# Four accumulator banks for the projection, and a new order of the last head's output projection, in a two-layer attention trunk

## The chip, the cores and the metric

The kernel runs on one core of one Trainium2 chip. The metric is the device time of one execution in microseconds (us). It was run three times before the change: 563.05, 563.07 and 563.96 us, median 563.07 us.

A core has a matrix engine (PE, which loads weights as PEld and multiplies as PE), a vector engine (DVE), an activation engine (ACT), a general engine (POOL) and a queue that starts transfers (SP). Each runs its own instruction list in order; the lists meet only at semaphores. PE writes its sums into eight banks (PSUM, 128 partitions of 512 floats each), which DVE and ACT read and write and POOL does not touch in this kernel.

## The reference, cut to what matters

```python
D_MODEL = 1024; SEQ = 512; DEPTH = 2; N_HEADS = 8; HEAD_DIM = 128
for i in range(DEPTH):                     # layer 0: MoBA with rotary; layer 1: forgetting attention
    hdn = rms_norm(x, norm_g[i])
    if i == 0:
        q, k, v, z = split(hdn @ a_w_in[0], 4)
        q = apply_rope(rms_norm(split_heads(q), a_q_norm)); k = apply_rope(rms_norm(split_heads(k), a_k_norm))
        y = moba_attention(q, k, v)        # two blocks of 256 and top-1 of the past block: plain causal attention
    else:
        q, k, v, z, f = parts of hdn @ b_w_in[0]
        log_f = log_sigmoid(f + b_f_bias); c = cumsum(log_f)
        q = rms_norm(q, b_q_norm); k = rms_norm(k, b_k_norm)
        y = softmax(causal(q @ k.T * d**-0.5 + c_q - c_k)) @ v
    x = x + (merge_heads(y) * silu(z)) @ w_out[i]
```

All products are computed in three matrix multiplications each (high part by high part, high by low, low by high), so that 32-bit inputs keep their precision.

## The kernel before, in words

The 512 tokens are four tiles of 128. A layer's input, normalised and turned, stays in `hT_hi` and `hT_lo`. The work goes head by head. For head h+1, `qkv` projects the four tiles: tile t is 24 matmuls of 384 columns (q, k and v) into one bank, and `zproj` is 24 matmuls of 512 columns for the gate z. ACT squares and sums q and k of a tile and copies v (`read_qkv`), POOL makes the reciprocal root (`rstd_qk`), and DVE applies it, with the rotation in layer 0 (`norm_qk`), and takes v's low part (`split_v`). When the four tiles are done, DVE turns q and k by 16 transposes into the two banks from QT_BANK (`turn_qk`), ACT and DVE split them into high and low parts (`split_qk`), and PE computes the scores of the head (`scores`) into banks 3, 4 and 5. DVE takes the row maxima (`maxima`), ACT the exponentials (`exps`), DVE inverts the sums (`invert_sums`), ACT scales (`normalise`), PE turns the probabilities (`turn_probs`) into banks 3, 4 and 5 again, ACT and DVE split them (`split_probs`), and PE multiplies by v (`values`, bank 3). DVE multiplies the result by the gate (`gate_y`), ACT and DVE split it (`split_y`, `low_y`).

Every engine has the same outer form (`heads_loop`): `first` for head 0's projection, one `period` written out, a loop of six more periods, and `last` for head 7. In period h PE does, in this order: the projection of head h+1's tiles 0 and 1, the scores of h, tiles 2 and 3, the turn of h's probabilities, z of h+1, the values of h. DVE's order is in `period` from line 1010, ACT's from line 723, POOL's from line 1144; they are fixed by hand and nothing overtakes.

Banks before: the projection alternates between banks 0 and 1 (head 0 of layer 0 has four), so tile t waits until `norm_qk` of tile t-2 has been through its bank. 2 is z, 3 is values and scores of tile 3, 4 and 5 the other scores, 6 and 7 the turned queries and keys. The statistics `ssq`, `rstd` have two slots. FORGET_BANK (4) is used once, at the head of layer 1.

`last` (PE line 532, DVE 1029, ACT 739) has no projection of a next head to set beside head 7's attention. In its place stand parts of the output projection: column half 0 for tiles 0, 1, 2, 3, of which the contributions of heads 0 to 6 can be summed early (a `project` for one tile and one head k is three matmuls of 512 columns), and head 7's contribution when `ylo_set` reports its low part. ACT in `last` converts weight chunks of the second half (`split_w`, four raw buffers): chunk 4 needs the buffer of chunk 0, which is loaded again when POOL has made chunk 0's low part.

Of the kernel before, what the change touches and what calls it, by code (L numbers as in the profile page):

```python
# [51 lines left out]
def build_trunk(nc, x, norm_g, w_out, a_w_in, a_q_norm, a_k_norm, b_w_in, b_f_bias, b_q_norm,  # L52
                b_k_norm, rope_cos, rope_sin, out):
    with ExitStack() as ctx:
# [42 lines left out]
        ssq = sb("ssq", [P, 2, 2])  # L97
        msq = sb("msq", [P, 2, 2])
        rstd = sb("rstd", [P, 2, 2])
# [7 lines left out]
        Z_BANK, Y_BANK, QT_BANK = 2, 3, 6  # L107
# [81 lines left out]
        def qkv_bank(layer, h, t):  # L189

            return (0, 1, 3, 4)[t] if layer == 0 and isinstance(h, int) and h == 0 else t % 2
# [7 lines left out]
        def turn_bank(layer, t):  # L199

            return 3 if layer == 0 and t == 1 else QT_BANK

        def unit_bank(c, t):

            return QT_BANK if c == 0 and t == 3 else t
# [6 lines left out]
                      (QT_BANK, t, slice(cols.start + CH // 2, cols.stop))]  # L212
# [125 lines left out]
        def _(pe):  # L338
# [51 lines left out]
            def qkv(layer, h, slot, t):  # L390

                a = TILES * (HEADS * layer + h) + t
                wait(pe, qkn_set, a - 1)
                if isinstance(a, int) and a == TILES:
                    for k in range(KC):
                        first_w(1, k)
                        qkv_part(layer, h, slot, t, (k,))
                    return
                if t == 0:
                    pe.wait_ge(wlo_set, KC * (JOBS * layer + h + 1))  # L400
                qkv_part(layer, h, slot, t, range(KC))
# [130 lines left out]
            def last(layer):  # L532
                g = HEADS * (layer + 1)
                u = TILES * OUT_CHUNKS * layer
                h = HEADS - 1

                pe.wait_ge(wlo_set, KC * (JOBS * layer + HEADS + 1))
                pe.wait_ge(ylo_set, g - 2)
                pe.wait_ge(qkn_set, TILES * g)
                project(layer, 0, 0, range(6), True, False)  # L540
                project(layer, 0, 1, range(2), True, False)
                scores(layer, h, 1)
                project(layer, 0, 1, range(2, 6), False, False)
                pe.wait_ge(ylo_set, g - 1)
                project(layer, 0, 0, [6], False, False)
                project(layer, 0, 1, [6], False, False)
                project(layer, 0, 3, range(5), True, False)
                turn_probs(layer, h)
                project(layer, 0, 3, range(5, 7), False, False)
                pe.wait_ge(gate_set, g)  # L550
                project(layer, 0, 2, range(3), True, False)
                values(layer, h, 1)
                project(layer, 0, 2, range(3, 7), False, False)
                pe.wait_ge(ylo_set, g)
                for t in range(TILES):
                    project(layer, 0, t, [h], False, True)
                pe.wait_ge(wlo_set, KC * (JOBS * layer + HEADS + 2))
                for t in range(TILES):
                    pe.wait_ge(x_added, u + 1 + t)
                    if layer + 1 == LAYERS and t == TILES - 1:  # L560
                        for part in out_parts[-2:]:
                            project_part(*part)
                    else:
                        project(layer, 1, t, range(HEADS), True, True)
                    if layer + 1 < LAYERS and t >= 1:
                        turn_hidden(layer + 1, t - 1)
# [6 lines left out]
        def _(act):  # L573
# [45 lines left out]
            def read_qkv(layer, h, s, t):  # L619
# [3 lines left out]
                wait(act, rstd_set, a - 1)  # L623
                wait(act, ssq_set, a)
                for m in range(2):
                    sq = act.activation(junk[:, m, :], banks[:, qkv_bank(layer, h, t), m * P:(m + 1) * P],  # L626
                                        ACT.Square, scale=SCALE, accum_out=ssq[:, t % 2, m:m + 1])
# [132 lines left out]
        def _(dve):  # L760
# [57 lines left out]
            def norm_qk(layer, h, t):  # L818
# [4 lines left out]
                if layer == 1:  # L823
                    for m in range(2):
                        last = dve.scalar_tensor_tensor(out=qkn[:, t, m, :], in0=banks[:, qkv_bank(layer, h, t), m * P:(m + 1) * P],
                                                        scalar=rstd[:, t % 2, m:m + 1], in1=cos_t[:, 0, m, :],
# [3 lines left out]
                for m in range(2):  # L830
                    swapped = banks[:, qkv_bank(layer, h, t), m * P:(m + 1) * P].rearrange("p (a n) -> p a n", a=2)[:, ::-1, :]
                    dve.scalar_tensor_tensor(out=rot[:, t % 2, m].rearrange("p (a n) -> p a n", a=2), in0=swapped,
                                             scalar=rstd[:, t % 2, m:m + 1],
# [3 lines left out]
                for m in range(2):  # L837
                    part = banks[:, qkv_bank(layer, h, t), m * P:(m + 1) * P]
                    dve.scalar_tensor_tensor(out=part, in0=part, scalar=rstd[:, t % 2, m:m + 1], in1=cos_t[:, t, m],
# [5 lines left out]
            def turn_qk(layer, h):  # L845

                g = HEADS * layer + h
                dve.wait_ge(qkn_set, TILES * (g + 1))
                for a in range(QUADS):
# [179 lines left out]
            def last(layer):  # L1029
                h = HEADS - 1  # L1030
                begin(layer, h)
                silu_part(layer, h, 0)
                maxima(layer, h)
                silu_part(layer, h, 1)
                invert_sums(layer, h)
                for n in range(2, 4):
                    silu_part(layer, h, n)
# [20 lines left out]
        def _(pool):  # L1058
# [17 lines left out]
            def rstd_qk(layer, h, t):  # L1076
                a = TILES * (HEADS * layer + h) + t
                pool.wait_ge(ssq_set, a + 1)
                wait(pool, qkn_set, a - 1)
                pool.tensor_tensor(msq[:, t % 2, :], ssq[:, t % 2, :], eps[:, :], ALU.add).then_inc(msq_set, 1)  # L1080
                pool.wait_ge(msq_set, a + 1)
                pool.tensor_tensor(rstd[:, t % 2, :], msq[:, t % 2, :], power[:, :], ALU.pow).then_inc(rstd_set, 1)  # L1082
# [122 lines left out]
```

## Time and profile before

| | us |
|---|---|
| median of three runs | 563.07 |
| the profiled execution, its own time | 564.51 |
| its span, first to last instruction | 562.5 |
| PE busy / PEld busy | 545.7 / 499.9 |
| DVE busy | 408.6 |
| ACT busy | 286.6 |
| POOL busy | 294.1 |

The busy time of PE is over matmuls that overlap each other, and their ends are modelled, so 97% does not mean that PE loses only 3%. A view that lists waits says for each engine which instruction waited and what released it; the view in order of time gives start, duration, engine, source line and operation, and in square brackets the idle time before it and its releaser. Most of the span is made of fourteen nearly equal periods, seven in each layer, and of two `last` sections, which begin near 236 us and 510 us.

### The profile page before, as it was taken

How to read it: one execution, taken by the hardware profiler on the slowest of the kernel's cores; microseconds unless marked ns; L12 is line 12 of the kernel's file. 1: busy time of each engine (PE TensorE's matmuls, PEld its weight loads, DVE VectorE, ACT ScalarE, POOL GpSimd, SP SyncE). 2: the span in 40 equal slices, each digit the busy share in tenths (PEclk: the TensorE clock that was granted, in tenths of full speed). 3: DMA queues.
4: the chain of work that ended last, by engine and by line, in shares of the span. 5: the costliest groups of instructions: out<-in, count | busy, mean ns of one | idle time of the engine just before them, and what ended most of it. 6: DMA issues, size and time to landing. Idle time of an engine off the chain costs nothing.

```text
span 562.5 us, 9740 instructions
## 1 busy us (share of the span) xinstructions
PE 545.7 (97%) x2958; PEld 499.9 (89%) x2958; DVE 408.6 (73%) x1039; ACT 286.6 (51%) x841; POOL 294.1 (52%) x348
## 2 busy tenths in 40 slices
PE   6998999999999999999999989999999999999998
PEld 4997999999999999878888989999999999998887
DVE  3799797979797979774363767787869595959321
ACT  5735555555454546453445463736464647373500
POOL 4854545454544444425545576657475756663700
PEclk9999999999999999999999999999999999999999
DMA  9812323131313131204442334423341535141221
GB/s 280 215 49 87 93 58 95 56 95 56 93 56 93 56 93 56 93 8 130 108 102 76 95 90 80 95 76 79 90 112 56 118 50 131 37 131 37 76 93 57
DMA packets 78237, 49.95 MB, mean 89 GB/s; under 512 B 4089, under 2 KB 71417, under 8 KB 78210
## 3 DMA queue, kind: packets, MB, share of 16 engines
q1 hardware_dynamic: 78208, 49.61, 32.6%
q8 instruction: 14, 0.23, 0.2%
q14 instruction: 13, 0.11, 0.1%
q10 hardware_dynamic: 2, 0.00, 0.0%
HBM read 47.48 MB, written 2.11 MB: 88 GB/s over the span
## 4 chain that ended last, share of the span: by engine, by line
PE 52%; DVE 17%; POOL 12%; issue 12%; ACT 3%; DMA 2%; SPq 1%; POOLq 0%; ACTq 0%; DVEq 0%
PE banks L343 14%; PE banks L345 14%; PE banks L344 14%; DVE banks L853 11%; POOL w_lo L1064 8%; PE banks L458 3%; POOL rstd L1082 3%; DVE pT_lo L894 2%; PE banks L444 2%; PE banks L375 1%; DMA w_raw<-in_b_w_in_dram 1%; POOL msq L1080 1%; DMA first_raw<-in_a_w_in_dram 1%; ACT junk L626 1%; PE banks L433 1%
## 5 line engine op out<-in xcount | busy, mean ns | idle before, releaser
L1064 POOL TENSOR_TENSOR w_lo<-w_raw,w_hi 128x512 fp32r<-128x512 f32 x147 | 188.4, 1300 | 94.8 <-ACT w_hi L590 94.8
L343 PE MATMUL banks<-w_hi,hT_hi 128*128 128x384 f32 x512 | 175.2, 342 | 8.7 <-DVE qkn L842 4.6
L345 PE MATMUL banks<-w_hi,hT_lo 128*128 128x384 f32 x512 | 172.2, 336 | 0.0
L344 PE MATMUL banks<-w_lo,hT_hi 128*128 128x384 f32 x512 | 172.2, 336 | 0.0
L853 DVE STREAM_TRANSPOSE banks<-qkn 32x256 f32<-32x256 f32 x256 | 116.6, 456 | 3.5
L343 PEld LDWEIGHTS banks<-w_hi,hT_hi 128*128 128x128 f32 x512 | 96.8, 189 | 13.1 <-DVE qkn L842 7.3
L590 ACT ACTIVATE w_hi<-w_raw 128x512 fp32r<-128x512 f32 x148 | 87.8, 643 | 21.8 <-DMA w_raw<-in_b_w_in_dram 13.9
L344 PEld LDWEIGHTS banks<-w_lo,hT_hi 128*128 128x128 f32 x512 | 97.0, 189 | 0.7
L345 PEld LDWEIGHTS banks<-w_hi,hT_lo 128*128 128x128 f32 x512 | 96.8, 189 | 0.0
L1080 POOL TENSOR_TENSOR msq<-ssq,eps 128x2 f32<-128x2 f32 x64 | 13.9, 218 | 125.0 <-ACT junk L626 125.0
L919 DVE RECIPROCAL gz<-gz 128x128 f32<-128x128 f32 x64 | 58.1, 928 | 0.0
L626 ACT ACTIVATE junk<-banks 128x128 bf16<-128x128 f32 x128 | 34.1, 276 | 41.2 <-PE banks L345 41.1
L635 ACT ACTIVATE qkT_hi<-banks 128x512 fp32r<-128x512 f32 x32 | 17.4, 596 | 72.5 <-DVE banks L853 72.5
L343 PE MATMUL banks<-w_hi,yT_hi 128*128 128x512 f32 (+1 forms) x136 | 51.9, 381 | 0.0
L642 ACT ACTIVATE probs<-probs,negmax 128x512 f32<-128x512 f32 (+1 forms) x64 | 35.2, 552 | 32.2 <-DVE negmax L878 32.2
L345 PE MATMUL banks<-w_hi,yT_lo 128*128 128x512 f32 (+1 forms) x136 | 51.3, 377 | 0.0
L344 PE MATMUL banks<-w_lo,yT_hi 128*128 128x512 f32 (+1 forms) x136 | 51.2, 377 | 0.0
L343 PE MATMUL banks<-hT_hi,w_hi 128*128 128x512 f32 x128 | 51.2, 400 | 0.0
L345 PE MATMUL banks<-hT_hi,w_lo 128*128 128x512 f32 x128 | 50.0, 391 | 0.0
L344 PE MATMUL banks<-hT_lo,w_hi 128*128 128x512 f32 x128 | 49.9, 390 | 0.0
L1082 POOL TENSOR_TENSOR rstd<-msq,power 128x2 f32<-128x2 f32 x64 | 45.1, 705 | 5.0
L815 DVE TENSOR_TENSOR v_lo<-banks,v_hi 128x128 fp32r<-128x128 f32 x64 | 17.4, 274 | 37.6 <-ACT v_hi L629 37.6
(108 smaller groups left out, 877.5 us busy)
## 6 DMA issues: line engine op xcount, KB each, us to landing
w_raw<-in_b_w_in_dram SPq DMA_DIRECT2D x64, 256.0 KB, 4.0
w_raw<-in_a_w_in_dram SPq DMA_DIRECT2D x52, 256.0 KB, 2.9
w_raw<-in_w_out_dram SPq DMA_DIRECT2D x32, 256.0 KB, 2.9
first_raw<-in_a_w_in_dram SPq DMA_DIRECT2D x12, 256.0 KB, 5.6
cos_t<-c_rows SPq DMA_DIRECT2D x8, 256.0 KB, 3.7
out_dram<-xs SPq DMA_DIRECT2D x7, 256.0 KB, 2.0
xs<-in_x_dram SPq DMA_DIRECT2D x3, 512.0 KB, 5.8
xs<-in_x_dram SPq DMA_DIRECT2D x2, 256.0 KB, 2.9
```

The costliest lines, as they stand in the source:

```text
L343: pe.matmul(dst, ah, bh, start=first and m == 0, stop=False)
L344: pe.matmul(dst, ah, bl, start=False, stop=False)
L345: mm = pe.matmul(dst, al, bh, start=False, stop=last and m == n - 1)
L590: act.activation(w_hi[:, slot, k, :], raw, ACT.Copy).then_inc(whi_set, 1)
L626: sq = act.activation(junk[:, m, :], banks[:, qkv_bank(layer, h, t), m * P:(m + 1) * P], ACT.Square, scale=SCALE, accum_out=ssq[:, t % 2, ...
L635: act.activation(qkT_hi[:, m, :], banks[:, QT_BANK + m, :], ACT.Copy).then_inc(qkThi_set, 1)
L642: act.activation(part, part, ACT.Exp, bias=negmax[:, t:t + 1], scale=-1.0, accum_out=rowsum[:, t:t + 1]).then_inc(exp_set, 1)
L853: at = dve.transpose(turned[:, :, :, a * QUAD:(a + 1) * QUAD], tokens[:, :, :, b * QUAD:(b + 1) * QUAD])
L919: dve.reciprocal(part, part).then_inc(ez1_set, 1)
L1064: pool.tensor_tensor(w_lo[:, slot, k, :], raw, f32(w_hi[:, slot, k, :]), ALU.subtract).then_inc(wlo_set, by)
L1080: pool.tensor_tensor(msq[:, t % 2, :], ssq[:, t % 2, :], eps[:, :], ALU.add).then_inc(msq_set, 1)
L1082: pool.tensor_tensor(rstd[:, t % 2, :], msq[:, t % 2, :], power[:, :], ALU.pow).then_inc(rstd_set, 1)
```

## The change

The projection of every head gets four banks (0, 1, 6, 7), and statistics four slots; the waits on `qkn_set` and `rstd_set` in `qkv`, `read_qkv` and `rstd_qk` are relaxed to four tiles back. The turned queries and keys move to banks 4 and 5, which the scores and the turned probabilities also use; so `turn_qk` gets a wait for `split_probs` of the head before. What used bank 6 outside the loops gets the name SPARE_BANK and stays there, but for the turns of layer 1's input, which move to 4 and 5. In `last` the order on PE and DVE is new.

```diff
-        Z_BANK, Y_BANK, QT_BANK = 2, 3, 6
+        Z_BANK, Y_BANK, QT_BANK, SPARE_BANK = 2, 3, 4, 6
...
         def qkv_bank(layer, h, t):
-            return (0, 1, 3, 4)[t] if layer == 0 and isinstance(h, int) and h == 0 else t % 2
+            return (0, 1, 3, 4)[t] if layer == 0 and isinstance(h, int) and h == 0 else (0, 1, 6, 7)[t]
...
         def turn_bank(layer, t):
-            return 3 if layer == 0 and t == 1 else QT_BANK
+            if layer == 1:
+                return QT_BANK
+            return 3 if t == 1 else SPARE_BANK
...
             def qkv(layer, h, slot, t):
                 a = TILES * (HEADS * layer + h) + t
-                wait(pe, qkn_set, a - 1)
+                wait(pe, qkn_set, a - TILES + 1)
...
                 project(layer, 0, 0, range(6), True, False)
-                project(layer, 0, 1, range(2), True, False)
+                project(layer, 0, 1, range(6), True, False)
                 scores(layer, h, 1)
-                project(layer, 0, 1, range(2, 6), False, False)
                 pe.wait_ge(ylo_set, g - 1)
-                project(layer, 0, 0, [6], False, False)
-                project(layer, 0, 1, [6], False, False)
-                project(layer, 0, 3, range(5), True, False)
+                for t in range(2):
+                    project(layer, 0, t, [6], False, False)
+                project(layer, 0, 3, range(7), True, False)
+                pe.wait_ge(gate_set, g)
+                project(layer, 0, 2, range(2), True, False)
                 turn_probs(layer, h)
-                project(layer, 0, 3, range(5, 7), False, False)
-                pe.wait_ge(gate_set, g)
-                project(layer, 0, 2, range(3), True, False)
+                project(layer, 0, 2, range(2, 7), False, False)
                 values(layer, h, 1)
-                project(layer, 0, 2, range(3, 7), False, False)
                 pe.wait_ge(ylo_set, g)
                 for t in range(TILES):
                     project(layer, 0, t, [h], False, True)
...
             def turn_qk(layer, h):
                 dve.wait_ge(qkn_set, TILES * (g + 1))
+                wait(dve, pTlo_set, 3 * g)
...
             def last(layer):              # DVE
                 begin(layer, h)
-                silu_part(layer, h, 0)
+                for n in range(4):
+                    silu_part(layer, h, n)
                 maxima(layer, h)
-                silu_part(layer, h, 1)
                 invert_sums(layer, h)
-                for n in range(2, 4):
-                    silu_part(layer, h, n)
                 split_probs(layer, h)
...
             def rstd_qk(layer, h, t):     # and read_qkv on ACT with rstd_set
-                wait(pool, qkn_set, a - 1)
+                wait(pool, qkn_set, a - TILES + 1)
```

## Rows read from the trace of the kernel before

**Rows 1.** Chain of waits from 66 to 240 us, shares by engine and line.

```profile
by line: issue 33.5%; DVE banks L853 25.2%; POOL w_lo L1064 18.2%; POOL rstd L1082 5.9%; DVE pT_lo L894 5.5%; POOL msq L1080 2.7%; ACT junk L626 2.2%; ACT qkT_hi L635 1.9%; DVE banks L839 1.4%; DVE rot L832 1.4%; POOLq L179 0.8%; ACTq L622 
```

**Rows 2.** Waits, PEld: us in total, times, longest.

```profile
PEld banks L343 <- DVE qkn L842: 7.3, 14, 1.5
```

**Rows 3.** DVE and ACT in time, one layer 0 period: start, us, instruction, idle before.

```profile
198.14 0.25 ACT L626 ACTIVATE junk<-banks 128x128 bf16<-128x128 f32 x1
...
198.93 0.29 DVE L815 TENSOR_TENSOR v_lo<-banks,v_hi 128x128 fp32r<-128x128 f32 x1 [1.43 <-ACT v_hi L629]
200.56 0.61 DVE L832 SCALAR_TENSOR_TENSOR rot<-banks,rstd,sin_t 128x128 f32<-128x128 f32 x2 [1.34 <-POOL rstd L1082]
202.74 0.61 DVE L832 SCALAR_TENSOR_TENSOR rot<-banks,rstd,sin_t 128x128 f32<-128x128 f32 x2 [0.26 <-POOL rstd L1082]
203.38 0.62 DVE L839 SCALAR_TENSOR_TENSOR banks<-banks,rstd,cos_t 128x128 f32<-128x128 f32 x2
...
204.38 1.61 DVE L894 TENSOR_TENSOR pT_lo<-banks,pT_hi 128x512 fp32r<-128x512 f32 x3
205.91 7.49 DVE L853 STREAM_TRANSPOSE banks<-qkn 32x256 f32<-32x256 f32 x16
```

**Rows 4.** Stretches, one period of layer 0 and one of layer 1: us, busy time per engine.

```profile
178.50:206.60 28.10, 27.53 (x155) 25.88 (x154) 24.53 (x68) 15.30 (x48) 13.65 (x16) 1.00 0.26 76
400.50:427.60 27.10, 27.10 (x156) 25.84 (x155) 20.86 (x56) 15.30 (x48) 17.06 (x22) 1.00 0.32 86
```

**Rows 5.** PE and PEld in time, layer 0's `last`.

```profile
243.45 0.19 PEld L431 LDWEIGHTS banks<-qkT_hi 128*128 128x128 f32 x1 [1.69 <-DVE qkT_lo L860]
257.52 0.56 PE L458 MATMUL banks<-pT_hi,v_hi 128*128 128x512 f32 x2
262.24 0.19 PEld L343 LDWEIGHTS banks<-w_hi,yT_hi 128*128 128x128 f32 x1 [0.34 <-DVE yT_lo L909]
```

**Rows 6.** DVE and ACT in time, the same section.

```profile
243.92 0.95 DVE L919 RECIPROCAL gz<-gz 128x128 f32<-128x128 f32 x1
244.79 0.69 DVE L878 CUSTOM_DVE_ANT_0 probs<-banks,strip 128x512 f32<-128x512 f32 x1
...
249.70 0.69 DVE L923 TENSOR_TENSOR gz<-banks,gz 128x512 f32<-128x512 f32 x1
255.39 1.62 DVE L894 TENSOR_TENSOR pT_lo<-banks,pT_hi 128x512 fp32r<-128x512 f32 x3 [5.00 <-ACT pT_hi L651]
...
249.53 2.18 ACT L590 ACTIVATE w_hi<-w_raw 128x512 fp32r<-128x512 f32 x4
254.25 0.63 ACT L590 ACTIVATE w_hi<-w_raw 128x512 fp32r<-128x512 f32 x1 [2.53 <-DMA w_raw<-in_w_out_dram]
```

**Rows 7.** Layer 1's first period in time: PEld, PE, DVE, POOL.

```profile
333.83 0.19 PEld L343 LDWEIGHTS banks<-w_hi,hT_hi 128*128 128x128 f32 x1 [2.29 <-DVE qkn L825]
...
346.29 0.56 PE L458 MATMUL banks<-pT_hi,v_hi 128*128 128x512 f32 x2
...
342.13 1.61 DVE L894 TENSOR_TENSOR pT_lo<-banks,pT_hi 128x512 fp32r<-128x512 f32 x3
...
340.61 0.19 POOL L1080 TENSOR_TENSOR msq<-ssq,eps 128x2 f32<-128x2 f32 x1 [0.75 <-ACT junk L626]
```

**Rows 8.** A stretch behind that stall; the last three columns are granted clock, DMA share, GB/s.

```profile
336.00:337.00 1.00, 1.00 (x5) 1.00 (x4) 0.00 (x0) 1.00 (x7) 0.60 (x1) 0.50 0.85 215
```

**Rows 9.** PE and DVE in time, layer 1's `last`.

```profile
530.09 0.56 PE L458 MATMUL banks<-pT_hi,v_hi 128*128 128x512 f32 x2
532.00 0.39 PE L343 MATMUL banks<-w_hi,yT_hi 128*128 128x512 f32 x1
534.73 0.39 PE L343 MATMUL banks<-w_hi,yT_hi 128*128 128x512 f32 x1
...
527.63 1.62 DVE L894 TENSOR_TENSOR pT_lo<-banks,pT_hi 128x512 fp32r<-128x512 f32 x3 [4.81 <-ACT pT_hi L651]
533.60 0.69 DVE L909 TENSOR_TENSOR yT_lo<-gz,yT_hi 128x512 fp32r<-128x512 f32 x1 [0.70 <-ACT yT_hi L663]
```

More of the change, by code:

```diff
@@ L96, in build_trunk @@
         msx = sb("msx", [P, TILES])
-        ssq = sb("ssq", [P, 2, 2])
+        ssq = sb("ssq", [P, TILES, 2])
         msq = sb("msq", [P, 2, 2])
-        rstd = sb("rstd", [P, 2, 2])
+        rstd = sb("rstd", [P, TILES, 2])
         power = sb("power", [P, 2])
@@ L199, in turn_bank @@
         def turn_bank(layer, t):
-            return 3 if layer == 0 and t == 1 else QT_BANK
+            if layer == 1:
+                return QT_BANK
+            return 3 if t == 1 else SPARE_BANK
         def unit_bank(c, t):
-            return QT_BANK if c == 0 and t == 3 else t
+            return SPARE_BANK if c == 0 and t == 3 else t
         out_parts = [(unit_bank(c, t), t, slice(c * CH, (c + 1) * CH)) for c in range(OUT_CHUNKS) for t in range(TILES)]
@@ L211, in build_trunk @@
         out_parts += [(bank, t, slice(cols.start, cols.start + CH // 2)),
-                      (QT_BANK, t, slice(cols.start + CH // 2, cols.stop))]
+                      (SPARE_BANK, t, slice(cols.start + CH // 2, cols.stop))]
         sin_flat = sin_t[:, :, :, :].rearrange("p a b n -> p (a b n)")
@@ L622, in read_qkv @@
                 act.wait_ge(a_done, a + 1)
-                wait(act, rstd_set, a - 1)
+                wait(act, rstd_set, a - TILES + 1)
                 wait(act, ssq_set, a)
@@ L626, in read_qkv @@
                     sq = act.activation(junk[:, m, :], banks[:, qkv_bank(layer, h, t), m * P:(m + 1) * P],
-                                        ACT.Square, scale=SCALE, accum_out=ssq[:, t % 2, m:m + 1])
+                                        ACT.Square, scale=SCALE, accum_out=ssq[:, t, m:m + 1])
                 sq.then_inc(ssq_set, 1)
@@ L825, in norm_qk @@
                         last = dve.scalar_tensor_tensor(out=qkn[:, t, m, :], in0=banks[:, qkv_bank(layer, h, t), m * P:(m + 1) * P],
-                                                        scalar=rstd[:, t % 2, m:m + 1], in1=cos_t[:, 0, m, :],
+                                                        scalar=rstd[:, t, m:m + 1], in1=cos_t[:, 0, m, :],
                                                         op0=ALU.mult, op1=ALU.mult)
@@ L832, in norm_qk @@
                     dve.scalar_tensor_tensor(out=rot[:, t % 2, m].rearrange("p (a n) -> p a n", a=2), in0=swapped,
-                                             scalar=rstd[:, t % 2, m:m + 1],
+                                             scalar=rstd[:, t, m:m + 1],
                                              in1=sin_t[:, t, m].rearrange("p (a n) -> p a n", a=2),
@@ L838, in norm_qk @@
                     part = banks[:, qkv_bank(layer, h, t), m * P:(m + 1) * P]
-                    dve.scalar_tensor_tensor(out=part, in0=part, scalar=rstd[:, t % 2, m:m + 1], in1=cos_t[:, t, m],
+                    dve.scalar_tensor_tensor(out=part, in0=part, scalar=rstd[:, t, m:m + 1], in1=cos_t[:, t, m],
                                              op0=ALU.mult, op1=ALU.mult).then_inc(rot_set, 1)
@@ L1078, in rstd_qk @@
                 pool.wait_ge(ssq_set, a + 1)
-                wait(pool, qkn_set, a - 1)
-                pool.tensor_tensor(msq[:, t % 2, :], ssq[:, t % 2, :], eps[:, :], ALU.add).then_inc(msq_set, 1)
+                wait(pool, qkn_set, a - TILES + 1)
+                pool.tensor_tensor(msq[:, t % 2, :], ssq[:, t, :], eps[:, :], ALU.add).then_inc(msq_set, 1)
                 pool.wait_ge(msq_set, a + 1)
-                pool.tensor_tensor(rstd[:, t % 2, :], msq[:, t % 2, :], power[:, :], ALU.pow).then_inc(rstd_set, 1)
+                pool.tensor_tensor(rstd[:, t, :], msq[:, t % 2, :], power[:, :], ALU.pow).then_inc(rstd_set, 1)
             pool.memset(one[:, :], 1.0).then_inc(ones_row, 1)
```

## The prediction, made before the change was run

> **What bounds the kernel now.** I read the chain of waits first, then the list of waits, then single periods in order of time. The change is about PE's waits for a bank, so the first question is whether these waits set the pace of layer 0. The list has 14 of them on the weight loads, 7.3 us in total [rows 2]: 1.7 us in layer 0's first period and six times 0.94 us in its loop. But in the chain from 66 to 240 us no line of PE appears among those shown; it runs through DVE's transposes, POOL's low parts and reciprocal roots, and a little ACT [rows 1]. The periods in order of time say why. DVE is idle three times in a period: 1.43 us for ACT's v copy of tile 2, 1.34 and 0.26 us for POOL's roots [rows 3]. ACT came to tile 2's squares at 198.14 without idling [rows 3]: it was busy with the head's probabilities and weight chunks, while PE had finished the tile before. So DVE waits for ACT and POOL, these wait for DVE, and the ring closes without PE. The layer 0 period is 28.10 us with DVE busy 24.53; layer 1's is 27.10 with PE busy 27.10 and DVE 20.86 [rows 4]. Layer 0 is paced by the ring, layer 1 by PE, and PE's wait for a bank in layer 0 is where the surplus of 1 us shows.
>
> Three places are left in which PE itself is on the path: its 1.69 us before layer 0's last scores [rows 5], its 2.29 us in layer 1's first period [rows 7], and the two `last` sections.
>
> **The change part by part**, in the time of the profiled execution (span 562.5, itself 564.5, runs 563.07).
>
> *Four banks, layer 0's loop.* PE arrives 0.94 us earlier at the turn and at z, and then waits that long for `pTlo_set` before `values`, because the ring sends it as before. Value 0; the lower end is that all 7.3 us [rows 2] come off, the upper 0. The relaxed waits on ACT and POOL sit behind work that is later anyway: 0.
>
> *The wait in `turn_qk`.* It is satisfied by DVE's own instruction just before. Without a wait the transposes begin at 205.91, 0.08 us before the last split ends (204.38 + 1.61); with a wait between two DVE operations the second starts 0.03 us behind the first (202.74 + 0.61 to 203.38) [rows 3]. That is 0.11 us more, on the ring, for heads 1 to 7: +0.8 us at the end of layer 0. Bounds 0 and 1.6 (twice that). Queued behind it are the 16 transposes, and behind these everything of the next head. In layer 1 DVE has 6 us to spare and it costs nothing. The Trainium skill, "VectorE: DVE Perf Modes", The DRAIN you can't avoid, says that a semaphore between DVE operations costs nothing extra; by that page the term would be 0 and the sum 0.8 lower. The overlap in the rows speaks against it.
>
> *`last` of layer 0.* A matmul of the output projection costs 0.2275 us (12 from 532.00 to 534.73) [rows 9].
> 1. Twelve of them, 2.73 us, move ahead of the scores and fill the wait of 1.69 us; PE's lead into this section gets 0.2 us shorter (`values` of head 6 starts behind the ring). Scores at 245.0, 1.5 late.
> 2. DVE does three more reciprocals (0.87 each from start to start) and the gate product (0.69) before the maxima [rows 6]. With the 0.8 they begin 2.62 + 0.69 + 0.8 = 4.1 us late, at 248.9; the late scores cost nothing beside that. The exponentials and the scaling shift by the same 4.1; the turn, at 254.4, just finds them done (253.8).
> 3. Queued behind the scaling on ACT are weight chunks 0 to 3, then chunk 4, then the split of the probabilities. Chunk 4 waits for its load, which waits for POOL's low part of chunk 0: 4.72 us from 249.53 to 254.25, of it 2.53 idle [rows 6]. This chain keeps its length, so DVE's last split ends not at 257.01 (255.39 + 1.62) but at 261.1, and `values` starts at 261.2 instead of 257.52 [rows 5]: +3.7, of it 2.2 us a wait that was not there.
> 4. Head 7's gate product, split and low part take as long as before, but the 12 matmuls (2.73 us) that PE did meanwhile now stand ahead. The 0.34 us wait before head 7's contribution [rows 5] becomes 2.7. That contribution starts at 266.0, +3.8 in all with the 0.8; 3.0 of this section's own.
> Bounds of its own part: 0.7, if the split of the probabilities does not come late (only the scores' 1.5 less the 0.8), to 4.5. I take 3.0, as each link has its row. Layer 1's first transfers hang on the same `ylo_set`, so they keep step.
>
> *Layer 1's first period.* PE's 2.29 us wait [rows 7] is for tile 1's norm, which is late behind the mask on POOL. With four banks tile 3 goes on at once. After the stall the granted clock fell to 0.50 [rows 8], the lower level of 1.2 GHz, from 335.0 to 338.2; some ten matmuls took 0.32 us instead of 0.17, 1.5 us. Both are gone, 3.8 us up to the turn. `values` then waits for the split of the probabilities: it ended at 343.74 and gets only the 0.75 us earlier that POOL waited for tile 3's squares [rows 7], 343.0. So `values` starts at 343.1 instead of 346.29 [rows 7]: -3.1. In an execution in which the clock did not fall there, -1.6; the profiled execution is 1.4 us slower than the median, so that may be the usual case. Bounds -3.8 and -1.
>
> *Layer 1's loop* is PE's own work: 0, bounds -0.5 and +0.5.
>
> *`last` of layer 1.* There was no wait before the scores, so they move 2.73 us later with the 12 matmuls. DVE's split, which ended at 529.25 [rows 9], comes 3.3 us later, at 532.6; PE arrives at 530.09 + 2.73 = 532.8 [rows 9] and does not wait. But the low part of head 7's result came at 533.60 + 0.69 = 534.29 behind `values` that ended at 532.00, and the 2.73 us of cover up to 534.73 [rows 9] are gone: 532.00 + 2.73 + 2.35 = 537.1, +2.4. Bounds 2.0 and 4.
>
> *Clock.* PE's new idle stretches are 2.2 and 2.7 us in the first `last`, 2.2 in the second. An idle stretch of 2.29 us was followed by the lower clock, one of 1.69 was not. A fall costs 1.2 to 1.6 us (1.5 as worked out above; in layer 0's `last` about 0.3 of it goes into a wait). I take one fall, 1.4; bounds 0 and 3.
>
> Sum: 0 + 0.8 + 3.0 - 3.1 + 0 + 2.4 = +3.1, with one fall +4.5. Against the median, where layer 1's gain may be 1.6 and not 3.1, +6.0. Between the two, nearer to the first: +4.7, 567.8 us.
>
> **The rivals.**
> *The banks pay in full.* PE is busy 97% of the span and loses the same gap in every period of layer 0. For it speaks only that PE is the busiest engine; against it the chain. It would give all of the 7.3 us: 4.7 - 7.3 = -2.6, and without a clock fall -4: 560 us. This is the case that the Trainium skill names in "Perfetto Trace Analysis", Optimization Strategy: consistent bubbles can mean that there is not enough PSUM. By that page the 0.94 us would be gained; the stretches [rows 4] show the gap, the chain [rows 1] that it is not the limit.
> *The `last` of layer 0 is mild.* If chunk 4's load does not hold up the split of the probabilities, this section costs 0.7; with the rest 0.8 + 0.7 - 3.1 + 2.4 = +0.8: 563.9 us. Against it: 2.53 us of idle for that very load [rows 6].
> *The clock falls in both `last` sections:* +3.1 + 1.2 + 1.6 = +5.9 and up to +7.4 without the old fall: 569.7 us. The idle stretches are like the one that was followed by a fall.
>
> **How the numbers follow.** Forecast 0.57, both falls 0.23, mild 0.11, banks in full 0.09. The time is that of the first, 567.8 us. The range 563.9 to 570.6 reaches from the mild case to both falls with the upper ends. About 0.2% (1.1 us) is what the runs can tell from no change. Faster comes from the full gain, 0.09; within 0.2% half of the mild case, 0.06; slower 0.85.
>
> **What would show it.** In the profile after: layer 0 periods of 28.1 to 28.2 us, with PE's wait for the norm gone and one of about 1 us for `pT_lo` in its place; no wait of PE before layer 0's last scores; a 2 us wait before its `values`; a wait of over 2 us for `yT_lo` in both `last` sections; layer 1's first stall gone. A layer 0 period near 27.2 us would make me wrong at the root; `values` of head 7 at an unchanged distance from the scores, in the largest term.

## The result, and the profile after

| | before | after | forecast |
|---|---|---|---|
| median, us | 563.37 (563.05 to 563.96, 4 runs) | 571.0 (568.46 to 573.39, 4 runs) | 567.8 (563.9 to 570.6) |
| ratio | | 1.0134, 95% interval 1.0089 to 1.0178 | 1.008 |
| profiled execution, us | 564.51 | 571.14 | |
| its span, us; mean granted clock | 562.5; 0.997 | 569.4; 0.988 | |

The direction was right, the size was not: +7.6 us instead of +4.7, and 0.4 us above the top of the range.

The page's first part, for the whole span: PE is busy for 96% and every other engine at most three quarters.

```profile
span 569.4 us, 9777 instructions
PE 548.2 (96%) x2958; PEld 501.3 (88%) x2958; DVE 409.6 (72%) x1039; ACT 286.0 (50%) x841; POOL 294.0 (52%) x348
```

The chain of waits from 66 to 240 us, by line, as [rows 1], and the waits on the weight loads (total, times, longest), which stand against [rows 2]:

```profile
by line: issue 28.9%; DVE banks L854 25.0%; POOL w_lo L1063 19.4%; POOL rstd L1081 5.1%; DVE pT_lo L895 4.4%; ACT junk L626 4.2%; ACT w_hi L590 4.2%; ACT qkT_hi L635 1.9%; POOL msq L1079 1.7%; DVE banks L839 1.4%; DVE rot L832 1.4%; POOLq L
```

```profile
PEld banks L460 <- DVE pT_lo L895: 10.6, 8, 2.4
PEld banks L345 <- DVE yT_lo L910: 5.5, 2, 2.9
```

The 7.3 us of waiting for `qkn` [rows 2] are gone from the list. Of the 10.6 us for `pT_lo`, 7.4 lie in layer 0's loop and stand in their place (six waits of 1.07 to 1.32 us); the other two are 2.39 us in layer 0's `last` and 0.79 in layer 1's first period. The same ring of DVE, POOL and ACT sets the pace, and PE now waits at `values`.

One period of layer 0 and one of layer 1, as [rows 4]. The third row is the time at which the clock was low before [rows 8], and the line behind it is head 0's `values` in layer 1 [rows 7]. Layer 1 begins some 6 us later now, so the third row alone does not settle that the fall is gone; but there is no wait of PE for a norm in layer 1's first period, and from 271 to 539 us the granted clock is 1.00 throughout.

```profile
92.88:121.08 28.20, 27.55 (x157) 25.88 (x156) 24.61 (x69) 15.19 (x48) 13.64 (x17) 1.00 0.26 75
413.00:440.00 27.00, 27.00 (x156) 25.76 (x155) 20.83 (x56) 15.30 (x48) 17.00 (x21) 1.00 0.32 87
335.00:338.30 3.30, 3.30 (x21) 3.30 (x20) 1.90 (x11) 2.62 (x9) 3.30 (x3) 1.00 0.21 58
```

```profile
349.25 0.30 PEld L460 LDWEIGHTS banks<-pT_hi,v_hi 128*128 128x128 f32 x2 [0.79 <-DVE pT_lo L895]
```

The period is the old one, a tenth of a microsecond longer. DVE in one of these periods: its three idle times are those of [rows 3] to 0.02 us, and between the split of the probabilities and the transposes there are 1.64 us (121.08 to 122.72) where there were 1.53 (204.38 to 205.91).

```profile
115.64 0.29 DVE L815 TENSOR_TENSOR v_lo<-banks,v_hi 128x128 fp32r<-128x128 f32 x1 [1.42 <-ACT v_hi L629]
117.25 0.61 DVE L832 SCALAR_TENSOR_TENSOR rot<-banks,rstd,sin_t 128x128 f32<-128x128 f32 x2 [1.32 <-POOL rstd L1081]
119.44 0.61 DVE L832 SCALAR_TENSOR_TENSOR rot<-banks,rstd,sin_t 128x128 f32<-128x128 f32 x2 [0.27 <-POOL rstd L1081]
...
121.08 1.61 DVE L895 TENSOR_TENSOR pT_lo<-banks,pT_hi 128x512 fp32r<-128x512 f32 x3
122.72 7.50 DVE L854 STREAM_TRANSPOSE banks<-qkn 32x256 f32<-32x256 f32 x16
```

Layer 0's `last` in time, as [rows 5, 6]: PE's loads, then DVE and ACT.

```profile
261.73 0.30 PEld L460 LDWEIGHTS banks<-pT_hi,v_hi 128*128 128x128 f32 x2 [2.39 <-DVE pT_lo L895]
266.38 0.29 PEld L345 LDWEIGHTS banks<-w_hi,yT_hi 128*128 128x128 f32 x1 [2.91 <-DVE yT_lo L910]
```

```profile
245.42 3.38 DVE L920 RECIPROCAL gz<-gz 128x128 f32<-128x128 f32 x4
248.84 0.69 DVE L924 TENSOR_TENSOR gz<-banks,gz 128x512 f32<-128x512 f32 x1
249.45 0.69 DVE L879 CUSTOM_DVE_ANT_0 probs<-banks,strip 128x512 f32<-128x512 f32 x1
...
260.05 1.62 DVE L895 TENSOR_TENSOR pT_lo<-banks,pT_hi 128x512 fp32r<-128x512 f32 x3 [7.38 <-ACT pT_hi L651]
...
254.19 2.18 ACT L590 ACTIVATE w_hi<-w_raw 128x512 fp32r<-128x512 f32 x4
258.90 0.63 ACT L590 ACTIVATE w_hi<-w_raw 128x512 fp32r<-128x512 f32 x1 [2.53 <-DMA w_raw<-in_w_out_dram]
```

Layer 1's `last`, as [rows 9]:

```profile
539.93 0.29 PEld L345 LDWEIGHTS banks<-w_hi,yT_hi 128*128 128x128 f32 x1 [2.60 <-DVE yT_lo L910]
```

PE now has three idle stretches of over 2 us in the two sections, and behind them the clock is low. The stretches with their granted clock in the third column from the end (0.50 is the lower level of 1.2 GHz):

```profile
264.00:270.00 6.00, 3.83 (x10) 2.84 (x10) 2.73 (x4) 0.63 (x1) 1.14 (x1) 0.50 0.31 96
540.00:543.50 3.50, 3.50 (x9) 2.79 (x10) 1.29 (x2) 0.00 (x0) 0.00 (x0) 0.53 0.09 33
```

The other low stretches of this execution last 3.3 us each, so I read more than six microseconds on end as two falls in a row: the first behind the wait for `pT_lo` that ended at 261.73, the second behind the wait for `yT_lo`, through which PE stood still at the low clock. A fourth fall, at 48 to 52 us, lies where the ring hides it.

The account of the profiled execution, as the distance of like instructions from those before: 0.55 us at the start (the first turn at 38.67 against 38.12), 1.38 behind head 6's split (233.81 against 232.43), 4.15 at head 7's contribution (266.39 against 262.24), 6.2 at 283.01, where PE turns layer 1's input, 2.96 at layer 1's first `values` (349.25 against 346.29), 5.2 at the last contribution (539.93 against 534.73), 6.9 at the end.

### The profile page after: what moved, and what is told of

The parts are those of the page before. It is cut to its first block, busy times and chain, and to the rows that moved or that the text cites. A ratio compares the mean times of both kernels' runs of the same rounds, so it can differ in the third digit from the quotient of the medians.

```text
span 569.4 us, 9777 instructions
## 1 busy us (share of the span) xinstructions
PE 548.2 (96%) x2958; PEld 501.3 (88%) x2958; DVE 409.6 (72%) x1039; ACT 286.0 (50%) x841; POOL 294.0 (52%) x348
## 4 chain that ended last, share of the span: by engine, by line
PE 45%; DVE 18%; POOL 15%; issue 11%; ACT 6%; DMA 2%; SPq 2%; POOLq 0%; ACTq 0%; DVEq 0%
PE banks L345 12%; PE banks L346 12%; PE banks L347 12%; DVE banks L854 11%; POOL w_lo L1063 9%; PE banks L460 3%; POOL rstd L1081 3%; DVE pT_lo L895 2%; DMA sin_t<-in_rope_sin_dram 2%; ACT w_hi L590 2%; ACT junk L626 1%; PE banks L446 1%; SPq L260 1%; POOL msq L1079 1%; DVE gz L920 1%
## 5 line engine op out<-in xcount | busy, mean ns | idle before, releaser
L345 PE MATMUL banks<-w_hi,hT_hi 128*128 128x384 f32 x512 | 173.2, 338 | 1.2 <-DVE hT_lo L796 1.2
L345 PE MATMUL banks<-w_hi,yT_hi 128*128 128x512 f32 (+1 forms) x136 | 53.5, 393 | 4.3 <-DVE yT_lo L910 4.3
L346 PE MATMUL banks<-w_lo,yT_hi 128*128 128x512 f32 (+1 forms) x136 | 52.5, 386 | 0.0
```

The source lines that it names most:

```text
L345: pe.matmul(dst, ah, bh, start=first and m == 0, stop=False)
L346: pe.matmul(dst, ah, bl, start=False, stop=False)
```

## The experiments

Each kernel was timed beside the kernel before on the same chip, in three groups: the first four below, with a median of before of 563.45 us; fill, the two short rings and best_last, with 563.18; after_act and the three of the last ring, with 562.8. Ratios are to these. The changed kernel's 571.0 was taken beside 563.37, so differences in microseconds from one group to another are good to about half a microsecond. Each diff is against the kernel named in front of it. The mean granted clock of an execution tells how often the clock fell: with no fall it is 1.0, and a fall takes 0.003 off (one stretch of 3.3 us at 0.50 in 563). Before's 56 timed executions of these groups show what one costs: 42 with 1.0 have the median 562.91, 13 with 0.997 have 564.43, 1.5 us more (the last has 0.994).

**banks_only**, from after: the whole order on PE and DVE in `last` as before, of which the diff shows the first lines.

```diff
-                project(layer, 0, 1, range(6), True, False)
+                project(layer, 0, 1, range(2), True, False)
                 scores(layer, h, 1)
+                project(layer, 0, 1, range(2, 6), False, False)
...
```

> The changed kernel with both engines' old order in the last section: four banks, shared banks for the turned queries, relaxed waits and the new wait stay. Theory A (ring of DVE, ACT and POOL paces layer 0; the cost of the change is all in the two last sections): layer 0 periods of 28.19 us (28.07 before), PE waiting some 1 us for pT_lo in each instead of for the norm, +0.8 us at the end of layer 0; layer 1's first stall and its clock fall gone, -1.6 to -3.1; no wait over 2 us in the last sections. Time 561.0 to 562.8 us against 563.4. Theory B (sharing banks or the new places of the projection cost time themselves): 566 us or more.

562.44 us (561.24 to 565.41, 12 runs), 0.9983 (0.9969 to 0.9996). The banks and the wait together gain 1.0 us of the 7.3 of [rows 2] (by the interval, 0.2 to 1.7), about what layer 1's first period gives (1.6) less the wait (0.8). In its profile the waits for the norm turn into waits for the split:

```profile
PEld banks L460 <- DVE pT_lo L897: 9.9, 8, 1.4
PEld banks L433 <- DVE qkT_lo L863: 4.2, 2, 2.3
```

```profile
92.80:120.99 28.19, 27.27 (x155) 25.67 (x154) 24.60 (x68) 15.25 (x48) 13.62 (x17) 1.00 0.26 75
```

One expectation was missed: with four banks and the old order PE waits 2.27 us for `qkT_lo` before layer 0's last scores, where it waited 1.69 before [rows 5], and in this execution the clock is low behind it (0.57 from 246 to 250 us). So the gap that the new order of `last` was to fill has grown with the banks.

**wait_only**, from before:

```diff
                 dve.wait_ge(qkn_set, TILES * (g + 1))
+                wait(dve, pTlo_set, 3 * g)
```

> The kernel before with only the satisfied wait for pT_lo in front of the 16 transposes. Theory A: 0.11 us more in each layer 0 period (28.07 to 28.18), +0.8 us in all, 564.1 to 564.3 us. Rival (a semaphore between two DVE operations costs nothing): 563.3 us, periods unchanged.

564.22 us (563.54 to 565.67, 12 runs), 1.0013 (1.0003 to 1.0023). At a clock of 1.0 its median is 563.79 (9 runs) against 563.07 of before in the same group (16 runs): 0.7 us, about the seven times 0.11 of the forecast. The period is 28.18 us with two banks, 28.19 with four in banks_only: in layer 0's loop the banks themselves change nothing.

**last_only**, from before: the new order of `last` on PE and DVE, with two banks and no wait.

```diff
-                project(layer, 0, 1, range(2), True, False)
+                project(layer, 0, 1, range(6), True, False)
...
-                silu_part(layer, h, 0)
+                for n in range(4):
+                    silu_part(layer, h, n)
                 maxima(layer, h)
...
```

> The kernel before with only the new order of the last section, on PE and DVE. Theory A: both new waits of each last section appear (2 us for pT_lo in layer 0, over 2 us for yT_lo in both), with the clock falling behind them: 3.0 + 2.4 of waits and 3.6 of falls on top of the time before, and layer 1's old stall stays: 570 to 573 us, as slow as the whole change or slower. Theory B (the cost sits in the banks, the last sections are mild): under 566 us.

569.43 us (567.86 to 571.76, 4 runs), 1.0116 (1.0088 to 1.0143). That is a little under the 570 to 573 expected. The order alone costs 6.0 us, most of the price of the change. Its executions lie by the clock: 567.86 at 1.0, 568.81 and 570.05 at 0.997, 571.76 at 0.993. So in the one execution without a fall the order costs 567.86 - 563.07 = 4.8 us (forecast: 3.0 + 2.4 = 5.4). The parts do not quite add up: 6.0 here and -1.0 in banks_only make 5.0, and the whole change costs 7.6. The profiles differ in two ways. PE waits 1.70 us for `pT_lo` here and 2.39 in after, and the clock falls once here and four times in after, once of it where the ring hides it. No run separates the two.

**old_dve_order**, from after: DVE's order in `last` as before, PE's new.

```diff
-                for n in range(4):
-                    silu_part(layer, h, n)
+                silu_part(layer, h, 0)
                 maxima(layer, h)
+                silu_part(layer, h, 1)
                 invert_sums(layer, h)
+                for n in range(2, 4):
+                    silu_part(layer, h, n)
```

> The changed kernel with only DVE's old order in the last section (first maxima after one silu part); PE's order stays new. Theory A: the wait of 2.0 us for pT_lo before layer 0's last values shrinks under 0.5 us since the weight chunk chain starts 2.5 us earlier; the waits for yT_lo, 2.2 us, stay in both sections. Time 567.5 to 569.5 us against 571.0. Rival (chunk 4 is late for another reason than the order on DVE): 570.5 to 571.5 us.

567.51 us (565.93 to 569.61, 4 runs), 1.0086 (1.0064 to 1.0108). The wait before head 7's `values` is gone from layer 0's section (layer 1's had none in after either), and the two waits for `yT_lo` are still there, 2.60 us each:

```profile
262.92 0.29 PEld L345 LDWEIGHTS banks<-w_hi,yT_hi 128*128 128x128 f32 x1 [2.60 <-DVE yT_lo L910]
```

This separates the two halves of the new order: DVE's costs 3.5 us (571.0 - 567.5), PE's 5.1 (567.51 - 562.44 of banks_only). PE's alone brings both `yT_lo` waits, and a fall with the first of them (granted clock 0.79 from 262 to 270). Behind the second, as long as the first, the clock does not fall in this execution.

**after_act**, from after: ACT splits the probabilities before it needs chunk 4.

```diff
-                split_w(layer, h + 2, 1, (0, 1, 2, 3, 4))
+                split_w(layer, h + 2, 1, (0, 1, 2, 3))
                 split_probs(layer, h)
-                split_w(layer, h + 2, 1, (5, 6, 7))
+                split_w(layer, h + 2, 1, (4, 5))
                 split_y(layer, h)
+                split_w(layer, h + 2, 1, (6, 7))
```

> The whole change, with ACT's last section reordered: the probabilities are split ahead of weight chunks 4 and 5, head 7's result ahead of 6 and 7. Theory A (the wait before the last values is the load of chunk 4, which stands ahead of the split, and its length varies): the 1.97 us wait for pT_lo in layer 0's last section goes, none of over 0.5 us appears in layer 1's whatever the load takes, the waits for yT_lo stay. Time 567.5 to 569 us against 571.0. Rival (the split is late because of the late maxima alone): wait and time as before, 570.5 us or more.

567.91 us (567.54 to 569.49, 6 runs), 1.009 (1.007 to 1.011). The wait for `pT_lo` before the last `values` is gone here too, with DVE's new order kept; so it was chunk 4 ahead of the split on ACT that passed DVE's delay on to PE. The `yT_lo` waits stay at 2.60, and all six executions have a clock of 0.994, two falls.

**fill**, from after: nine matmuls of 512 columns that nobody reads (2.2 us of work), into bank 7, where PE would stand still.

```diff
+                if layer == 0:
+                    fill(9)
                 values(layer, h, 1)
+                fill(9)
                 pe.wait_ge(ylo_set, g)
```

> The changed kernel with nine matmuls of 512 columns into the unused bank 7 (2.05 us of work whose result nobody reads) in each of PE's long waits of the last sections: before layer 0's last values, and before the wait for head 7's low part in both layers. Nothing on any other engine's path changes. Theory A (beyond the waits the clock falls in both last sections and costs 2.1 and 1.6 us): no granted clock of 0.50 near 264 and 540 us, time 566.5 to 568.0 us and a narrow spread. Rival (the excess over the forecast is waiting, the clock is a bystander): 570.5 to 572 us, as the matmuls put at the waits can only add.

568.49 us (566.27 to 569.19, 6 runs), 1.0089 (1.0068 to 1.011). The clock is 1.0 in all six, so the falls were part of the price and not a bystander; the time is 0.5 us above the 568.0 at which the expectation ended. The stretch behind the contribution, here and in after:

```profile
266.00:270.30 4.30, 4.17 (x19) 3.44 (x19) 2.86 (x5) 0.00 (x0) 0.00 (x0) 1.00 0.50 148
```

```profile
266.00:270.30 4.30, 3.91 (x9) 3.14 (x10) 1.72 (x3) 0.00 (x0) 0.00 (x0) 0.51 0.48 148
```

The number of records beside PE and PEld tells more than the busy time: 19 loads against 10 in the same 4.3 us. The executions did not have the narrow spread that was expected: they lie around 566.6 (two) and 568.7 (four). The profile of one of the four shows a possible reason: in layer 1's `last` chunk 4's load landed later than in after, counted from chunk 0, and `values` waited 2.10 us for the split behind it at 534.77. The two faster executions have no profile. ACT in fill, then in after:

```profile
525.17 2.18 ACT L598 ACTIVATE w_hi<-w_raw 128x512 fp32r<-128x512 f32 x4
531.95 0.63 ACT L598 ACTIVATE w_hi<-w_raw 128x512 fp32r<-128x512 f32 x1 [4.59 <-DMA w_raw<-in_w_out_dram]
```

```profile
527.93 2.18 ACT L590 ACTIVATE w_hi<-w_raw 128x512 fp32r<-128x512 f32 x4
532.45 0.63 ACT L590 ACTIVATE w_hi<-w_raw 128x512 fp32r<-128x512 f32 x1 [2.33 <-DMA w_raw<-in_w_out_dram]
```

The transfers of chunks 4 to 7 were issued at the same distance from ACT's chunk 0 in both, 2.02 us (at 527.19 and 529.95). So POOL's low part, which frees the buffer, was not late; the transfer itself was: from its issue to ACT's start on chunk 4 there are 4.8 us in fill and 2.5 in after.

**after_short_ring** and **before_short_ring**, from after and from before: DVE's reciprocal for the third quarter of the gate is one column wide in layer 0, 0.8 us less on the ring in each period. The kernels leave out the rest of that quarter, so their output is not the reference's.

```diff
+                if n == 2 and layer == 0:
+                    part = part[:, 0:1]
```

> The changed kernel with DVE's third reciprocal of each layer 0 head cut to one column (0.93 to about 0.15 us), so that the gate of a quarter of layer 0's tokens is wrong by that step. It stands before the maxima, on the ring. Theory A (the ring paces layer 0): periods of 28.19 fall by 0.75 to 27.4, time 5 to 6 us less than the whole change: 565 to 566.5 us. Rival (PE or the bank paces layer 0): periods fall by less than 0.3, time within 1.5 us of 571.

> The same cut in the kernel before. With two banks PE still waits for tile 0's norm before tile 2, which stands ahead of the cut, so part of the saving is kept from PE. Theory A: the ring wants 27.3 us, PE with its bank wait 27.1 plus about 0.7, so the period falls from 28.07 to between 27.4 and 27.9; time 558 to 562 us; the gap of the two kernels in layer 0's period shows what four banks are worth once the ring is shorter. Rival (the bank wait paces layer 0 already): period unchanged at 28.0 or more.

After: 563.6 us (561.77 to 566.85, 9 runs), 7.4 below the changed kernel, period 27.65. Before: 559.5 (558.87 to 560.0, 4 runs), 0.9942 (0.9922 to 0.9963), period 27.51. The shorter instruction is on DVE alone, and PE's time follows it in both kernels, so the ring paces layer 0. The period gives back 0.55 of the 0.8 us, less than the 0.75 expected: something else on the ring takes up the rest, and no run shows what. Seven periods explain 3.8 us each (7 times 0.55 in both). After gained more than the 5 to 6 us expected. In the profiles 1.1 us lie ahead of the first scores (47.10 against 48.17), 1.1 in layer 0's `last` up to head 7's contribution, where the third reciprocal now stands ahead of the maxima, and 1.6 behind layer 1's contribution, where the clock does not fall here.

**best_last**, from after: the twelve matmuls ahead of the scores stay, but are taken from between the scores and the turn, and not from behind `values`; DVE's order as before; chunk 4 behind the split.

```diff
-                project(layer, 0, 3, range(7), True, False)
-                pe.wait_ge(gate_set, g)
-                project(layer, 0, 2, range(2), True, False)
+                project(layer, 0, 3, range(5), True, False)
...
-                split_w(layer, h + 2, 1, (0, 1, 2, 3, 4))
+                split_w(layer, h + 2, 1, (0, 1, 2, 3))
                 split_probs(layer, h)
-                split_w(layer, h + 2, 1, (5, 6, 7))
+                split_w(layer, h + 2, 1, (4, 5, 6, 7))
```

> The changed kernel's banks with another last section: DVE's old order; PE puts the 12 matmuls ahead of the scores but takes them from the stretch between scores and turn, so that 15 stand before values and 12 behind as in the kernel before; ACT converts weight chunk 4 after the split of the probabilities. Theory A: the wait before the scores is filled, no new wait: about 1.3 us less than with the old last section: 560 to 561.5 us. Rival (the turn then waits for the probabilities, PE gains nothing): as the run with the old last section, 561.5 to 563 us.

564.39 us (562.34 to 566.57, 12 runs), 1.0025 (1.0008 to 1.0041): no gain, and above both the 560 to 561.5 us expected and the 563 at which the rival ended. The four chunks that ACT now converts between the split of the probabilities and head 7's result wait for three loads, and the result stands behind them at 260.66:

```profile
257.08 1.38 ACT L591 ACTIVATE w_hi<-w_raw 128x512 fp32r<-128x512 f32 x2 [2.30 <-DMA w_raw<-in_w_out_dram]
258.82 0.63 ACT L591 ACTIVATE w_hi<-w_raw 128x512 fp32r<-128x512 f32 x1 [0.36 <-DMA w_raw<-in_w_out_dram]
260.12 0.63 ACT L591 ACTIVATE w_hi<-w_raw 128x512 fp32r<-128x512 f32 x1 [0.67 <-DMA w_raw<-in_w_out_dram]
260.66 0.62 ACT L664 ACTIVATE yT_hi<-gz 128x512 fp32r<-128x512 f32 x1
```

PE then waits 1.01 us for `yT_lo` in layer 0 and 2.09 in layer 1, where banks_only has neither wait. That profile is of a fast execution without a fall (562.54); seven of the twelve have a clock below 1.0, and these lie from 564.26 to 566.57. How much of the miss is waiting and how much falling was not separated.

**ring_banks** and **before_ring**: the ring shortened with all its work kept, in banks_only and in before.

```diff
# ACT, period
-                split_w(layer, h + 2, s, (4,))
                 read_qkv(layer, h + 1, 1 - s, 2)
+                split_w(layer, h + 2, s, (4,))
# POOL, period
-                split_w(layer, h + 2, s, (3, 4))
+                split_w(layer, h + 2, s, (3,))
                 rstd_qk(layer, h + 1, 2)
-                split_w(layer, h + 2, s, (5,))
+                split_w(layer, h + 2, s, (4,))
                 rstd_qk(layer, h + 1, 3)
-                split_w(layer, h + 2, s, (6, 7))
+                split_w(layer, h + 2, s, (5, 6, 7))
```

> Four banks, the old order in the last section, and in the loop of both layers ACT reads tile 2 before it converts weight chunk 4, while POOL makes tile 2's and tile 3's roots one chunk earlier. This shortens the ring by some 1.4 us. Theory A (the ring paces layer 0, PE needs 27.1 us): layer 0's period falls from 28.19 to 27.1-27.3, time 6 to 7 us under the run without the reorder: 555 to 557 us. Rival (PE's own limit or the banks): period stays over 27.9.

> The same reorder of ACT and POOL in the kernel before, with its two banks. Theory A: with a ring shorter than PE's work the norms come before PE asks for the bank, as in layer 1, so two banks are enough: layer 0's bank waits vanish, period 27.1-27.4, time 556 to 558 us; four banks are then worth only layer 1's first period, 1 to 2 us. Rival (the bank wait is a limit of its own): the waits stay near 0.9 us in each period and the time stays above 560 us.

ring_banks: 553.28 us (552.29 to 553.74, 5 runs), 0.9819 (0.9798 to 0.984). before_ring: 558.77 (557.02 to 560.41, 6 runs), 0.9924 (0.99 to 0.9947). One period of layer 0, in ring_banks and in before_ring:

```profile
90.32:117.33 27.01, 27.01 (x155) 25.69 (x154) 24.59 (x68) 15.18 (x48) 13.62 (x17) 1.00 0.28 79
```

```profile
90.52:117.79 27.27, 27.27 (x156) 25.78 (x155) 24.59 (x69) 15.39 (x48) 13.68 (x17) 1.00 0.27 78
```

The busy times of DVE, ACT and POOL are those of [rows 4], and PE has no gap left: the ring was long by order, not by work. Both results missed their expectation: ring_banks is 1.7 us below the 555 to 557 us, before_ring 0.8 above the 556 to 558. So the four banks, worth 1.0 us in the old order (banks_only), are worth 5.5 here, more than the 1 to 2 that was expected. 1.4 us of it come up to head 7's `values` in layer 0 (250.33 against 251.73) and 3.3 in layer 1's first period (`values` 335.06 against 339.76, 4.7 in all), which keeps its stall with two banks, and a low clock behind it:

```profile
327.53 0.19 PEld L343 LDWEIGHTS banks<-w_hi,hT_hi 128*128 128x128 f32 x1 [2.26 <-DVE qkn L825]
```

```profile
325.00:331.00 6.00, 4.06 (x18) 3.74 (x17) 2.69 (x9) 4.40 (x15) 3.83 (x6) 0.81 0.88 200
```

Five of before_ring's six executions have a clock of 0.997, one fall; of ring_banks' five none is below 0.999. The one of before_ring at 1.0 took 557.02, so without the fall the banks are worth about 3.7 us, from a single execution.

**ring_last**, from ring_banks: PE's order of best_last and ACT's of after_act, of which the diff shows the last lines.

```diff
...
-                split_w(layer, h + 2, 1, (5, 6, 7))
+                split_w(layer, h + 2, 1, (4, 5))
                 split_y(layer, h)
+                split_w(layer, h + 2, 1, (6, 7))
```

> The shorter ring with four banks and a last section in which PE has the 12 matmuls ahead of the scores, 15 and 12 at their old places, DVE its old order and ACT the split of the probabilities and of head 7's result ahead of chunks 4-5 and 6-7. Theory A: as the ring leads PE, there is no wait before the scores to be filled, so PE's part gives nothing; ACT's part takes the chunk loads off the path and narrows the spread: 554.5 to 556.5 us, within 1 us of the run with the old last section. Rival (the fill before the scores is worth 1.7 us by itself): 2 us or more below that run.

551.37 us (550.62 to 552.21, 5 runs), 0.979 (0.9769 to 0.9811): 11.4 us below before, 19.6 below the changed kernel, and the best of all. Against ring_banks it is 1.9 us, more than the 1 expected and close to the rival's 2. In ring_banks PE waited 1.89 us before layer 0's last scores; here that wait is gone. ACT's order was changed in the same run, so the two shares are not separated. Against best_last's order, only chunks 4 and 5 stand ahead of the split of head 7's result, and in layer 0 they are done 1.20 us before its operand is there. Of its waits on the weight loads none but the start's is over 1.5 us.

## Why the prediction came out too low

*Four banks in layer 0's loop: 0.* Right. The waits moved from `qkn` to `pT_lo`, and the period did not shorten: 28.19 us in banks_only, 28.18 in wait_only. The rival that the banks pay in full is out (0.9983), and with it here the reading of the Trainium skill, "Perfetto Trace Analysis", Optimization Strategy, that consistent bubbles can mean too little PSUM. In a shorter ring that reading applies: ring_banks is 5.5 us below before_ring.

*The wait in `turn_qk`: +0.8.* Right: +0.83 between the start and head 6 in the profile, 0.7 in wait_only. By the Trainium skill, "VectorE: DVE Perf Modes", The DRAIN you can't avoid, it would have been 0; both runs speak against that. The section's sentence is on eight copies that took the same time with and without semaphores, and the same section says that a next operation that is not held starts earlier; that is the case here, and the wait takes it away.

*`last` of layer 0: scores at 245.0, maxima 248.9, `values` 261.2 behind a wait of 2.2, contribution 266.0.* Measured 245.7, 249.45, 261.73 behind 2.39, and 266.39. The chain through chunk 4's load was the right one (after_act takes it away). Less the 0.55 us of the start, the four are met within 0.2; the start's 0.55 was in no term and stays unexplained.

*Layer 1's first period: -3.1.* Right for the execution profiled: 6.2 to 2.96 is -3.2, with the stall and its low clock gone. But I knew that this term was -1.6 where before's clock does not fall there, and 42 of before's 56 executions are such. That is the first error, worth 1.3 us: for the median the sum was +6.0, not the +4.7 between the two. I leaned to the profiled execution because its rows were before me.

*`last` of layer 1: +2.4.* +2.2 measured.

*One fall of the clock, 1.4.* This is the step that failed. The waits were forecast to half a microsecond, what they do to the clock was not. The profile after has two falls in a row in layer 0's `last` and one in layer 1's, and behind the contributions they cost 2.06 (4.15 to 6.2) and 1.7 us (5.2 to 6.9): 3.8 instead of 1.4. Even the rival with a fall in both sections, 569.7, took 2.8. With the waits of the forecast, before's usual execution and this clock the sum is 0.8 + 3.0 - 1.6 + 2.4 + 3.8 = +8.4; the median moved 7.6. The four executions lie in order of their clock (568.46 at 0.997, 570.85 at 0.991, 571.14 and 573.39 at 0.988), but the last two are 2.2 us apart at the same clock, so the falls are not all that varies. By the same measure a single fall behind that contribution cost 1.8 us in old_dve_order and 1.9 in after_act: the pair in after costs hardly more than one, because PE stood still through much of its low clock. So two things were wrong in the term: the number of falls (one, where this profile has two in layer 0's section and one in layer 1's) and the price of one in layer 0's `last` (1.2 us in the rival, about 2 measured). fill, which keeps PE busy and has no fall, is 2.5 us lower as a median and 4.4 in its two fastest executions. If these are the ones in which chunk 4's load was not late, which no profile shows, that brackets the term.

*What I priced at one value and varies:* the load of chunk 4. ACT idled 2.53, 2.53, 2.33 and 4.59 us for the same transfer in four places. Before, PE did not wait for it; the new order has put it on the path, and the executions of fill spread over 2.9 us at one clock; but before's 42 executions at 1.0 spread over 2.2 us too, so the load is not shown to be the cause of the spread. In fill it was the transfer that was slow, not its issue; what slowed it is open.

## What to carry to other kernels

A wait of PE that repeats in every period is not evidence that PE's wait is the limit. Find the ring that sets the period and shorten it first (here by order alone, 28.1 to 27.3 us), and only then are more banks worth something: 1.0 us in the old order, 5.5 in the new (part of it a fall of the clock that the kernel with two banks has in layer 1's first period).

Work moved ahead of a wait is taken from somewhere. The twelve matmuls that filled a gap of 1.69 us had covered two later waits down to 0.34 us and nothing, and these came back at 2.9 and 2.6. Take it from where the engine has slack: the same twelve taken from between the scores and the turn cost nothing in ring_last. In best_last, with another order on ACT, they brought no gain.

Idle stretches of over 2 us on PE can cost twice here, once as waiting and once in the clock. Count them before and after, price each, and base the sum on the usual execution, not on the one that was profiled.

## What the hardware showed that I had not expected

The clock can fall twice on end: 264 to 270 us at 0.50 when a second idle stretch of 2.91 us lies within the first low stretch. A fall cost 1.5 us in before (564.43 against 562.91), 1.7 at the end of layer 1, 1.8 to 1.9 behind layer 0's contribution, and 2.1 there for the pair.

The length of an idle stretch does not decide alone whether the clock falls. The wait of 2.60 us for `yT_lo` in layer 1's `last` was followed by the lower clock in after and after_act and not in old_dve_order and last_only; the stall of 2.3 us in layer 1's first period was followed by it in the profiles of before and before_ring and not in those of wait_only and last_only.

Nine unread matmuls of 512 columns in each gap kept the clock at 1.0 in six of six executions; the changed kernel has no execution of four at 1.0.

A wait on DVE for a semaphore that the DVE instruction just before it sets costs 0.11 us where the two would otherwise overlap: 1.64 us against 1.53 from start to start, and 0.03 us behind the end of the split (121.08 + 1.61 to 122.72) instead of 0.08 ahead of it.
